# Queries of two mixers projected with stationary weights, 512 tokens moving, in a two-layer decoder trunk

## What is computed

```python
h = rms_norm(x, norm_mix_pre[i])
proj = h @ w_in[i]                       # 512 x 1024 times 1024 x 2688
a_u, a_v, b_q, b_k, b_v, b_g, c_q, c_k, c_v = split_cols(proj, IN_SIZES)
y_a = gmlp_mixer(a_u, a_v, ...)
y_b = retention_mixer(b_q, b_k, b_v, b_g, ...)   # 6 heads of 64, rope over all 64
y_c = swa_sink_mixer(c_q, c_k, c_v, ...)         # 6 query heads, 2 key heads, rope over 16
mix = jnp.concatenate([y_a, y_b, y_c], -1) @ w_out[i]
x = x + rms_norm(mix, norm_mix_post[i])
# then SwiGLU with d_ff 2816, and x + sigmoid(x @ w_gate) * rms_norm(p @ w_ple)
```

## Time and profile before

| | |
|---|---|
| median of 3 runs | 1225.6 us (1225.6 to 1225.62) |
| the profiled execution's own time | 1225.42 us |
| its span, first to last instruction | 1223.7 us |
| PE busy | 1217.0 us, 99% of the span |
| DVE, ACT, POOL busy | 841.5, 616.0, 136.6 us |
| moved by DMA | 122.31 MB, mean 100 GB/s |

### The profile page before, as it was taken

How to read it: one execution, slowest core, us unless ns; L and a number is a source line. 1 busy time by engine, 2 the same in 40 slices (tenths; PEclk the granted TensorE clock), 3 DMA queues, 4 the chain that set the end, 5 groups by cost and what they waited for, 6 DMA issues and landing times.

```text
span 1223.7 us, 20397 instructions
## 1 busy us (share of the span) xinstructions
PE 1217.0 (99%) x7873; PEld 1109.8 (91%) x7873; DVE 841.5 (69%) x1365; ACT 616.0 (50%) x1204; POOL 136.6 (11%) x208
## 2 busy tenths in 40 slices
PE   9999999999999999999999999999999999999998
PEld 8988888999999988888899889889999999888887
DVE  5685646888888853267976756468988887433788
ACT  7454435555555532237664544364655555422474
POOL 2003621100000000003030037020000000000120
PEclk9999999999999999999999999999999999999999
DMA  7322232233333354320242222231333333444001
GB/s 247 111 65 91 70 103 69 70 104 104 104 105 106 109 183 154 124 67 18 86 119 73 91 75 90 74 103 53 104 105 106 108 101 119 163 147 172 18 18 70
DMA packets 124464, 122.31 MB, mean 100 GB/s; under 512 B 5200, under 2 KB 108752, under 8 KB 124368
## 3 DMA queue, kind: packets, MB, share of 16 engines
q1 hardware_dynamic: 123680, 120.48, 31.4%
q10 hardware_dynamic: 688, 0.53, 0.2%
HBM read 118.90 MB, written 2.10 MB: 99 GB/s over the span
## 4 chain that ended last, share of the span: by engine, by line
PE 98%; DVE 1%; ACT 0%; POOL 0%; issue 0%; DVEq 0%; ACTq 0%
PE bank L1004 31%; PE bank L1006 30%; PE bank L1005 30%; PE bank L1214 2%; PE bank L1273 1%; PE bank L1294 1%; PE bank L1333 1%; PE bank L1317 1%; PE bank L1309 0%; PE bank L1281 0%; PE bank L1329 0%; PE bank L1338 0%; PE bank L1224 0%; PE bank L1359 0%; PE bank L1255 0%; DVE ple_n L2196 0%
## 5 line engine op out<-in xcount | busy, mean ns | idle before, releaser
L1004 PE MATMUL bank<-w_hi,h_hi 128*128 128x384 f32 (+2 forms) x564 | 200.4, 355 | 0.8 <-DVE w_lo L1893 0.7
L1005 PE MATMUL bank<-w_lo,h_hi 128*128 128x384 f32 (+2 forms) x564 | 194.6, 345 | 0.0
L1891 DVE TENSOR_TENSOR w_lo<-raw,w_hi 128x1024 fp32r<-128x1024 f32 x70 | 83.6, 1233 | 133.7 <-ACT w_hi L1411 133.5
L1004 PE MATMUL bank<-h_hi,w_hi 128*128 128x256 f32 x568 | 161.0, 284 | 0.1
L1006 PE MATMUL bank<-h_hi,w_lo 128*128 128x256 f32 x568 | 160.7, 283 | 0.0
L1005 PE MATMUL bank<-h_lo,w_hi 128*128 128x256 f32 x568 | 160.7, 283 | 0.0
L1006 PE MATMUL bank<-w_hi,h_lo 128*128 128x384 f32 (+2 forms) x468 | 157.5, 336 | 0.0
L1411 ACT ACTIVATE w_hi<-raw 128x1024 fp32r<-128x1024 f32 x70 | 70.6, 1053 | 160.7 <-PE bank L1006 160.6
L1006 PE MATMUL bank<-w_hi,mid_lo 128*128 128x512 f32 x352 | 137.0, 389 | 0.0
L1004 PE MATMUL bank<-T_hi,w_hi 128*128 128x256 f32 x448 | 126.8, 283 | 0.0
L1005 PE MATMUL bank<-T_lo,w_hi 128*128 128x256 f32 x448 | 126.8, 283 | 0.0
(11 more groups left out here) (294 smaller groups left out, 2909.3 us busy)
## 6 DMA issues: line engine op xcount, KB each, us to landing
raw<-in_w_ffn_in SPq DMA_DIRECT2D x88, 512.0 KB, 3.9
raw<-in_w_ffn_out SPq DMA_DIRECT2D x44, 512.0 KB, 4.2
raw<-in_w_in SPq DMA_DIRECT2D x40, 384.0 KB, 3.8
raw<-in_w_out SPq DMA_DIRECT2D x16, 512.0 KB, 3.8
gw<-in_w_gate SPq DMA_DIRECT2D x16, 512.0 KB, 3.4
raw<-in_w_in SPq DMA_DIRECT2D x10, 512.0 KB, 4.6
raw<-in_w_ple SPq DMA_DIRECT2D x4, 512.0 KB, 5.9
x<-in_x_in SPq DMA_DIRECT2D x3, 512.0 KB, 6.9
```

The costliest lines, as they stand in the source:

```text
L1004: pe.matmul(out_ap, a_hi, b_hi, start=start, stop=False, skip_group_check=True)
L1005: pe.matmul(out_ap, a_hi, b_lo, start=False, stop=False, skip_group_check=True)
L1891: last = dve.tensor_tensor(lo, raw[q % RAWS][:, cols], hi, ALU.subtract)
```

## The change

The queries of both mixers leave the old scheme. Their columns of `w_in` are moved next to each other on the host (`turned_last`, which also orders the `cq` heads in pairs) and form three groups of 256 columns, `qa`, `qb`, `qc`, one strip each. In these the weights are stationary (128 columns of them) and 512 tokens of `h` move. A block of 128 query columns is 24 matmuls and comes out transposed: six blocks, three for `cq` and three for `bq`. A unit of these strips is half a block, 12 matmuls of 512 columns. No transposes of queries are left: `swa_T` happens once for all four chunks (4 transposes of `ck`), `ret_T` has three transposes in place of six.

The rotation is done on the transposed block. ACT copies the block from PSUM to `q_raw`. Then its queue issues four DMAs that copy partitions to exchanged partitions of `q_turn` (8 or 32 partitions by 512 columns each; partitions that do not turn were set to zero by POOL). DVE multiplies `q_raw` by a table of cosines, `q_turn` by one of signed sines, and adds. The tables have a column for each token (4 tables of 128 x 512, loaded by SP in each layer, behind new waits in layer 1). The factor of the norm, which was a scale per token in the evacuation, now goes into the scale of the exponential (`s_q`) and of the maximum (`s_qn`), both made by POOL.

In layer 1 block 0 is done in two parts: 384 tokens ahead of the last `ckv` product (`q_most`, 24 matmuls of 384 columns), the last 128 tokens behind it (24 matmuls of 128 columns).

Units 4 to 15 are now `qa`, `qb`, `qc`, 16 to 23 `bk`, 24 to 31 `bv`, 32 to 39 `a`, 40 to 47 `bg`; the mixers' steps are placed anew.

```diff
-    "cq": (2 * AW + 4 * BW, BW),
-    "bk": (2 * AW + BW, BW),
-    "bq": (2 * AW, BW),
+    "qa": (2 * AW + 3 * BW, 2 * P),
+    "qb": (2 * AW + 3 * BW + 2 * P, 2 * P),
+    "qc": (2 * AW + 3 * BW + 4 * P, 2 * P),
+    "bk": (2 * AW, BW),
...
+    for i in range(2 * len(TURNED)):
+        put(6 + 2 * i, "q_rope", i)
+    put(8, "swa_T")
     for c in range(TILES):
-        put(10 + c, "swa_T", c)
-        u = (13, 18, 23, 28)[c]
+        u = (12, 16, 21, 26)[c]
         put(u, "swa_cur", c)
         if c:
             put(u + (1 if c < 3 else 2), "swa_yhi", c - 1)
         put(u + 1, "swa_prev", c)
         if c:
             put(u + (1 if c < 2 else 2), "swa_ylo", c - 1)
-        put(u + (2, 1, 2, 2)[c], "swa_norm", c)
-        put(u + 5, "swa_PT", c)
-        put(u + (5, 5, 3, 5)[c], "swa_mask", c)
-        put(u + 7, "swa_o", c)
+        put(u + (2, 2, 2, 1)[c], "swa_norm", c)
+        put(u + (4 if c == 0 else 5), "swa_PT", c)
+        put(u + (4 if c == 0 else 5), "swa_mask", c)
+        put(u + (6 if c == 0 else 7), "swa_o", c)
...
-        u = (33, 37, 41, 45)[c]
+        u = (30, 34, 38, 42)[c]
         for step, name in zip((0, 2, 3), ("ret_T", "ret_sc", "ret_o")):
             put(u + step, name, c)
...
             mm(ins[0], 2, nxt)
+            add("q_most", lay=nxt)
+            mm(ins[0], 3, nxt)
             mm(ins[1], 0, nxt)
             mm(ins[1], 1, nxt)
-            mm(ins[0], 3, nxt)
...
-ACT_EVAC = ["ckv", "cq", "bv", "a", "bg"]
-DVE_EVAC = ["bk", "bq"]
+ACT_EVAC = ["ckv", "bv", "a", "bg"]
+DVE_EVAC = ["bk"]
...
+            def mm_turned(layer, i, half, cols):
...
+                c = slice(i % 2 * P, i % 2 * P + P)
+                for k in range(4 * half, 4 * half + 4):
+                    last = mm3(banks[i % 4][:, cols], hi[:, k, c], lo[:, k, c], h_hi[:, k, cols], h_lo[:, k, cols],
+                               k == 0, k == KD - 1)
+                return last
...
-                    for i, src in enumerate((bk, bq)):
-                        for j in range(3):
-                            last = pe.transpose(banks[4 + i][:, j * P:(j + 1) * P],
-                                                src[:, c, j * P:(j + 1) * P], T_("ident"))
+                    for j in range(3):
+                        last = pe.transpose(banks[4][:, j * P:(j + 1) * P], bk[:, c, j * P:(j + 1) * P], T_("ident"))
...
+                        act.activation(q_raw[b][:], banks[i % 4][:, :], ACT.Copy).then_inc(q_evac, 1)
+                        act.wait_ge(q_evac, n)
+                        half = HD // 8 if i < 3 else HD // 2
+                        for r in (0, HD):
+                            for d in (r, r + half):
+                                src = 2 * r + half - d
+                                act.dma_start(q_turn[b][d:d + half, :],
+                                              q_raw[b][src:src + half, :]).then_inc(q_turned[b], 16)
...
+                elif kind == "q_rope":
...
+                    dve.tensor_tensor(dst, q_raw[b][:], cos_q[which][:], ALU.mult)
+                    dve.wait_ge(q_turned[b], 64 * (3 * layer + i // 2 + 1))
+                    step(dve.tensor_tensor(q_turn[b][:], q_turn[b][:], sin_q[which][:], ALU.mult))
+                    done(dve.tensor_tensor(dst, dst, q_turn[b][:], ALU.add), q_roped)
```

More of the change, by code:

```diff
@@ L388, in small_tables @@
     table = np.concatenate([np.eye(P), rc, rs, sc, ss, lower_t, qs, ks], 1)
-    return np.ascontiguousarray(table.astype(f)), later
+    turns = np.zeros((4, P, S), f)
+    for i, (half, theta) in enumerate(((HD // 8, 500000.0), (HD // 2, 10000.0))):
+        inv = (1.0 / (f(theta) ** (np.arange(half, dtype=f) / f(half)))).astype(f)
+        a = (pos[None, :] * inv[:, None]).astype(f)
+        turns[2 * i] = 1.0
+        for r in (0, HD):
+            turns[2 * i, r:r + half] = turns[2 * i, r + half:r + 2 * half] = np.cos(a).astype(f)
+            turns[2 * i + 1, r:r + half] = -np.sin(a).astype(f)
+            turns[2 * i + 1, r + half:r + 2 * half] = np.sin(a).astype(f)
+    return np.ascontiguousarray(table.astype(f)), later, turns
 TABLE_COLS = {}
@@ L402, in build_trunk @@
                 post_mix, pre_ffn, w_ffn_in, w_ffn_out, post_ffn, w_gate, w_ple, ple_norm,
-                table, later, out):
+                table, later, turns, out):
     KB = 1024
@@ L519, in build_trunk @@
     r_mix = [small(1) for _ in range(TILES)]
+    s_q = [small(1) for _ in range(TILES)]
+    s_qn = [small(1) for _ in range(TILES)]
     nsnk = small(C_HEADS)
@@ L579, in build_trunk @@
     ck_roped = sem("ck_roped")
-    cq_roped = sem("cq_roped")
+    turns_loaded = [sem(f"turns_loaded{i}") for i in range(2)]
+    q_evac = sem("q_evac")
+    q_turned = [sem(f"q_turned{i}") for i in range(2)]
+    q_roped = sem("q_roped")
+    q_scaled = sem("q_scaled")
+    q_zeroed = sem("q_zeroed")
     b_roped = sem("b_roped")
@@ L1161, in block_of @@
                     pe.wait_ge(lo_ready, 2 * (g + 1))
-                if kind == "in":
+                if kind == "in" and strip[1] in TURNED:
+                    block = 2 * TURNED.index(strip[1]) + m // 2
+                    last = mm_turned(layer, block, m % 2, slice(S - P if layer and block == 0 else 0, S))
+                elif kind == "in":
                     last = mm_in(layer, g, strip, m)
@@ L1246, in _ @@
                     gate_product(layer, e[1], e[2:] or (0, 1))
+                elif kind == "q_most":
+                    for half in range(2):
+                        mm_turned(layer, 0, half, slice(0, S - P))
                 elif kind == "swa_T":
-                    c = e[1]
-                    pe.wait_ge(ck_roped, layer * TILES + c + 1)
-                    pe.wait_ge(cq_roped, layer * TILES + c + 1)
-                    if c > 1:
-                        pe.wait_ge(swa_cT, layer * TILES + c - 1)
-                    for j in range(3):
-                        pe.transpose(banks[6 + c % 2][:, j * P:(j + 1) * P], cq[c % 2][:, j * P:(j + 1) * P],
-                                     T_("ident"))
-                    pe.transpose(banks[6 + c % 2][:, 3 * P:4 * P], ck[:, c, :],
-                                 T_("ident")).then_inc(swa_T, 1)
+                    pe.wait_ge(ck_roped, (layer + 1) * TILES)
+                    for c in range(TILES):
+                        last = pe.transpose(banks[6][:, c * P:(c + 1) * P], ck[:, c, :], T_("ident"))
+                    last.then_inc(swa_T, 1)
                 elif kind in ("swa_cur", "swa_prev"):
@@ L1313, in _ @@
                     c = e[1]
-                    pe.wait_ge(ret_kqT, layer * TILES + c + 1)
+                    pe.wait_ge(ret_kT, layer * TILES + c + 1)
+                    if c == 0:
+                        pe.wait_ge(q_roped, 6 * layer + 6)
                     for j in range(3):
                         for g in range(2):
-                            last = pe.matmul(banks[4 + g][:, j * P:(j + 1) * P], kqT[rows(g), 0, j, :],
-                                             kqT[rows(g), 1, j, :], start=True, stop=True,
+                            last = pe.matmul(banks[4 + g][:, j * P:(j + 1) * P], kT[rows(g), j, :],
+                                             qT[rows(g), j, ts(c)], start=True, stop=True,
                                              skip_group_check=True)
@@ L1699, in _ @@
                     act.wait_ge(ret_T, layer * TILES + c + 1)
[L1700 to L1704 removed]
+                    act.activation(kT[:], banks[4][:, 0:BW].rearrange("p (k t) -> p k t", k=3),
+                                   ACT.Copy).then_inc(ret_kT, 1)
                 elif kind == "ret_o":
@@ L2363, in _, with turned_last @@
                         dve.wait_ge(mm_done, mm_count(layer, strip, m))
-                        rope_full(layer, DVE_EVAC.index(name), m)
+                        rope_full(m)
+def turned_last(w):
+    a, bq, bk, bv, bg, cq, ckv = np.split(w, np.cumsum([2 * AW] + 5 * [BW]), 2)
+    cq = cq.reshape(*w.shape[:2], C_KV, C_HEADS // C_KV, HD).transpose(0, 1, 3, 2, 4).reshape(cq.shape)
+    return np.concatenate([a, bk, bv, bg, cq, bq, ckv], 2)
 def heads_in_pairs(w):
@@ L2385 @@
     depth = w_in.shape[0]
-    table, later = small_tables()
+    table, later, turns = small_tables()
     values = {
@@ L2396 @@
         "w_gate": w_ple_gate, "w_ple": w_ple_proj, "ple_norm": ple_norm,
-        "table": table, "later": later,
+        "table": table, "later": later, "turns": turns,
     }
```

127 lines of the change are left out of this document (79 added, 48 removed).

## The result

The changed kernel takes 1256.2 us (median, 1254.91 to 1257.22) against 1225.6 us before: ratio 1.0249, 95% interval 1.0232 to 1.0267. It is slower by 30.6 us, where 5.3 were forecast. Its profiled execution has a span of 1255.4 us, 31.7 us more than before.

A forecast was written before the change was run, and what follows sets the result against it. PE, busy 99% at full clock, was taken as the bound: -5.1 + 1.0 + 2 x (2.5 + 2.0 + 0.2) = +5.3 us, so 1230.9 us. Its own range was 1228.5 to 1233 us; with rivals, 1221.0 to 1235.0 us.

The forecast's parts named there:

- The sign: Whole kernel: the change makes it slower, by 5.3 us.
- two main mechanisms: PE waits in both layers for scores of `swa_prev` (2.5 us) and for `y_lo` at `ret_T` (2.0 us).
- PE's work: Query matmuls and transposes on PE: -0.57 us in layer 0, +0.78 in layer 1, -5.28 for transposes; -5.1 us.
- -5.28 us for transposes: Mixers: 12 transposes of `cq` and 12 of `bq` gone per layer, 48 x 0.11 us, counted in full.
- Start of layer 1: DVE's longer lo part of strip 1 delays `h_lo` of token tile 2, so PE waits 1.0 us, once.
- Unit 22: `swa_prev` of chunk 2: two rotations of `bk` ahead of DVE's mask make PE wait 2.5 us a layer.
- Unit 30: `ret_T` of chunk 0: longer 512-wide conversion delays DVE's `y_lo`; PE waits 2.0 us a layer, 0.7 to 2.4.
- The other waits: Exchange mostly covered; `swa_PT` of chunk 0, `swa_prev` of chunk 1, `swa_o` of chunk 0 without cover: 0.2 us a layer.
- The retention chain keeps its spacing: Retention steps in the mixers: no wait expected, and the shorter gap to `ret_yT` leaves over 4 us.
- A wait put onto PE lengthens it in full: Whole kernel: nothing hides behind another engine, so each PE wait is priced at its length, without a clock term.
- the late exchange: Rival: partition exchange lands late because it shares 16 DMA engines with the weights; +2.5 us, 1233.4 us; chance 0.06.
- The faster rival: The waits at `swa_prev` of chunk 2 and `ret_T` of chunk 0 don't bind: 1220.5 to 1221.5 us; chance 0.22.

The follow-up runs named there:

- the last experiment: Changed kernel with reordered mixer steps, a few conversions held back, and ACT issuing block 5's DMAs behind its copy of chunk 1's scores: 1224.0 us, ratio 0.9988.

## Why the prediction was wrong

The sign and the two main mechanisms were right, the size was wrong by a factor of six. Its own steps, one by one:

- **PE's work, -5.1 us.** Two terms were right to the hundredth. In the changed kernel's PE timeline the 128-column products start 0.1115 us apart ((651.63 - 649.40)/20; 0.11 was taken), and the 512-column ones 0.227 us:

```profile
649.40 0.27 PE L1034 MATMUL bank<-h_hi,w_hi 128*128 128x128 f32 x1
...
651.63 0.28 PE L1036 MATMUL bank<-h_hi,w_lo 128*128 128x128 f32 x1
```

  The sum is worth less than that. In the last experiment, which has few waits, the list of PE's waits is 1.3 us longer than before (4.1 to 2.8) and the span 1.4 us shorter, so the work is some 2.7 us less, not 5.1. The balance of the changed kernel gave 2.4.

  PE's timelines of before and of the last experiment show where the rest is. Priced by their width, the products of the projections come to +0.2 us, as forecast. What is off is the -5.28 us for transposes. Call what a mixer puts between two products of a projection a piece, and take its length from the start of the product ahead of it to the start of the one behind it, without the listed waits: all pieces together are 3.0 us shorter, not 5.3. Where a piece went from six transposes to three it is 0.33 us shorter, as priced (116.22 to 117.03 us before, 118.35 to 118.83 now). But the transposes of the four `swa_T` took 1.50 us a layer and the one `swa_T` of now takes 0.36, 1.14 saved and not 1.32. And nine pieces have short idle times which they hadn't before, 1.7 us in all. The list of waits leaves these out, as it counts from the modelled end of the last product, 0.34 us long at a spacing of 0.17. The largest ones are 0.3 us, such as this one in the last experiment, where 0.44 us pass between two starts:

```profile
73.46 0.34 PE L1048 MATMUL bank<-w_hi,h_lo 128*128 128x384 f32 x1
73.90 0.88 PE L1342 MATMUL bank<-tab,prob 128*128 128x128 f32 x6
```

- **Start of layer 1, +1.0 us.** Measured 0.88, from the cause given: in the runs that have `h_lo` ahead of that conversion this wait is gone.
- **Unit 22, +2.5 us a layer.** Mechanism right, size off: 3.05 and 3.07 us. The run without exchange has 1.95, so the exchange, which I had called covered, makes 1.1 us of it. How that divides between the issues (0.63 us each, 0.46 forecast) and DVE's waits for landing no run separates. The slower exponentials of chunk 1 (0.56 us) are in this chain too and had no term.
- **Unit 30, +2.0 us a layer.** Mechanism right, 2.76 and 2.77 us, above the upper value of 2.4. From DVE's first copy (101.71) to the end of the exponentials (107.33) are 5.6 us, where 4.9 was taken: 0.56 of this is the slower exponentials, which the prediction had left at their old price.
- **The other waits, 0.2 us a layer.** 0.6, 2.3 and 0.95 us came out for `cT`, chunk 0's probabilities and chunk 1's scores, 3.85 in all against 0.4. The last two are places named as having no cover. The first I had called covered, with 2.8 us left: ACT's copy of block 2 came behind the hi part of a conversion (39.21, 2.14 us long, the copy at 41.74), and with that conversion held back to unit 10 the wait is gone. The third place named, `swa_o` of chunk 0, has no wait in the changed kernel.
- **"The retention chain keeps its spacing".** This is the step that failed among the waits. The spacing is kept, but not the place of the strip's end in it. A conversion and the gMLP's sum, waiting for POOL, now stand ahead of chunk 2's scores: 5.0 us. The run with the scores one unit earlier showed it.
- **"A wait put onto PE lengthens it in full".** This is the step that failed most. A wait of 2.5 us and more costs its length and then 3.4 or 6.8 us at 1.2 GHz, which lose 1.7 or 3.4 us: 13.1 us in six places. I had read from the earlier trace rows that the clock was full and hadn't asked what kept it so: PE's longest wait behind the start was 0.46 us. The run with the long wait in the kernel before showed it by itself.

The difference of 26.4 us between forecast and trace, 31.7 to 5.3, is thus 13.1 of clock, 5.0 of the missed wait, 2.6 of the two undersized ones, 3.45 of the small ones, 2.7 of PE's own work, less 0.1 for layer 1 and 0.2 for a wait on weights that is gone from the start of layer 0: 26.5. The term of PE's own work is what the balance left over, so that the sum closes is no proof of it; the last experiment gives 2.4 for the same term.

Of the rivals, none had the result, and the late exchange (+2.5 us) was nearest to a real mechanism: taking the exchange away saved 9.4 us. The faster rival lacked the order; with that mended it comes out at 1224.0 us, not at 1220.5 to 1221.5, as the work saved is half of what was priced and 1.3 us more of waits are left.

## What to carry to other kernels

Where PE is busy for 99%, a transfer of work from PE to the other engines must be judged by the places where PE meets them: walk every such place, and at each write down what stands ahead on the engine waited for, the conversions at a strip's end above all. If a wait of some 2 us or more turns up, ask for the slow clock behind it as well (here it came behind every wait of 2.5 us and more and behind some of 1.8), as a full clock in the profile of before says nothing on a kernel with gaps. Price an instruction anew when one of its operands changes from a constant to a tile. And when a step is late, move what is needed first ahead; holding back every conversion left 1245.5 us here, holding back three of them 1229.1 us.
